# Routing of a two-layer decoder trunk: LayerNorm sums by VectorE, statistics and logits with tokens on partitions

## The reference

```python
h = _layer_norm(ALPHA * h + mix, ln_mix_g[layer], ln_mix_b[layer])   # mean, variance over the 1024 features
scores = jax.nn.sigmoid(jnp.einsum('bld,de->ble', h, w_router))      # 64 experts
biased = scores + router_bias
# 8 groups of 8 experts, the best 4 groups by the sum of their two best, the best 8 experts in them
w = ROUTED_SCALE * w / jnp.sum(w, axis=-1, keepdims=True)            # gates of the 8 chosen
```

## Time and profile before

| | us |
|---|---|
| median of 3 runs | 1601.27 |
| lowest, highest | 1598.33, 1609.75 |
| the profiled execution, its own time | 1615.54 |
| its span in the profile | 1613.8 |

### The profile page before, as it was taken

One profiled execution on the slowest core, in us unless ns is written; L12 is line 12 of the kernel. 1 busy time (PEld: TensorE's weight loads), 2 busy tenths in 40 slices (PEclk: granted clock), 3 DMA queues, 4 the chain that ended last, 5 costly groups with the idle time before them and its releaser, 6 DMA issues. The chain is left out here.

```text
span 1613.8 us, 24656 instructions
## 1 busy us (share of the span) xinstructions
PE 1461.5 (91%) x9414; PEld 864.6 (54%) x9414; DVE 691.3 (43%) x1471; ACT 355.4 (22%) x744; POOL 249.7 (15%) x323
## 2 busy tenths in 40 slices
PE   8999888999898999897999877987999997979996
PEld 6788668887544444353545466863434342424442
DVE  3889747631533343342434258043233332323323
ACT  3766454220410111110111020132011111111111
POOL 5779525200100000000000000001000000000000
PEclk9999999799899999898999978987999998989999
DMA  7679361039389999999999881395999999999994
GB/s 271 208 189 258 129 162 55 2 132 367 142 339 419 423 423 422 425 422 424 420 422 423 365 301 72 129 384 188 363 423 425 422 425 423 423 423 420 426 422 192
DMA packets 101490, 512.46 MB, mean 318 GB/s; under 512 B 36836, under 2 KB 42020, under 8 KB 66300
## 3 DMA queue, kind: packets, MB, share of 16 engines
q1 hardware_dynamic: 91548, 481.81, 75.3%
q0 software_dynamic: 9824, 29.05, 4.9%
HBM read 508.92 MB, written 17.10 MB: 326 GB/s over the span
## 5 line engine op out<-in xcount | busy, mean ns | idle before, releaser
L1986 DVE TENSOR_TENSOR e_ac<-e_sl,banks 128x256 f32<-128x256 f32 x54 | 22.7, 421 | 408.5 <-ACT e_sl L1895 408.5
L1774 PE MATMUL banks<-upper,e_xgT 128*64 128x512 f32 (+1 forms) x864 | 195.5, 612 | 1.3 <-issue 1.1
L304 PE MATMUL banks<-hT,dense_ring 128*128 128x272 f32 x768 | 184.9, 399 | 5.3 <-DMA dense_ring<-in_w_in 5.3
L1381 POOL DMA_INDIRECT x_xg<-rows_dram,x_idx x54 | 53.6, 993 | 848.6 <-DVE x_idx L1373 842.2
L1774 PE MATMUL banks<-dense_ring,e_xgT 128*64 128x512 f32 (+1 forms) x320 | 149.5, 623 | 38.3 <-issue 37.2
L304 PEld LDWEIGHTS banks<-hT,dense_ring 128*128 128x128 f32 x768 | 147.5, 193 | 39.3 <-DMA dense_ring<-in_w_in 5.3
L1774 PE MATMUL banks<-experts,e_xgT 128*64 128x512 f32 (+1 forms) x704 | 153.4, 608 | 0.9 <-issue 0.9
L1774 PEld LDWEIGHTS banks<-dense_ring,e_xgT 128*64 128x64 f32 (+1 forms) x320 | 41.1, 131 | 134.5 <-issue 132.5
L1895 ACT ACTIVATE e_sl<-banks 128x256 f32<-128x256 f32 x54 | 20.8, 385 | 402.4 <-PE banks L1774 402.4
L1792 PE MATMUL banks<-x_sg,route_consts 128*128 128x272 f32 x432 | 104.5, 394 | 2.8 <-ACT route_consts L1910 1.4
L1774 PEld LDWEIGHTS banks<-upper,e_xgT 128*64 128x64 f32 (+1 forms) x864 | 65.1, 132 | 74.4 <-issue 74.4
(11 more groups left out here) (453 smaller groups left out, 2179.0 us busy)
## 6 DMA issues: line engine op xcount, KB each, us to landing
upper<-in_moe_gate_up SPq DMA_DIRECT2D x54, 2048.0 KB, 25.2
experts<-in_moe_gate_up SPq DMA_DIRECT2D x44, 2048.0 KB, 26.9
upper<-in_moe_down SPq DMA_DIRECT2D x44, 1024.0 KB, 25.2
experts<-in_moe_down SPq DMA_DIRECT2D x44, 1024.0 KB, 26.2
dense_ring<-in_moe_down SPq DMA_DIRECT2D x40, 1024.0 KB, 25.0
dense_ring<-in_moe_gate_up SPq DMA_DIRECT2D x20, 2048.0 KB, 15.0
dense_ring<-in_w_in SPq DMA_DIRECT2D x47, 512.0 KB, 4.6
x_gate_up<-in_moe_gate_up SPq DMA_DIRECT2D x10, 2048.0 KB, 19.2
```

The costliest lines, as they stand in the source:

```text
L304: mm = pe.matmul(ps[g % 4][:, 0:T], slot[:, n % SLOTS_IN, c, :], hT[:, c, :], start=(c == 0), stop=(c == DC - 1))
L1381: pool.indirect_dma_start(out=ex["xg"][:, i % 2, :], out_offset=None, in_=mem["rows_dram"], in_offset=bass.IndirectOffsetOnAxis(ap=ex["idx ...
L1774: mm = pe.matmul(gub[e * n:(e + 1) * n, :], xgT[:, i % 2, c, e * n:(e + 1) * n], gate_up_weights(mem, j)[:, c, :], start=(c == 0), stop=(c ...
L1986: dve.tensor_tensor(ac[:], sl[:], gub[:, FF:], ALU.mult).then_inc(mul, 1)
```

## The change

Layer statistics move ahead: while the mixer's last projection runs, ScalarE squares each finished tile and VectorE adds up tiles and squares elementwise (`tally`, two adds per tile, one tile behind). The column sums go. The router's weight product, its column sum and its bias row are made in the same stage, on GpSimd and TensorE. In the routing stage TensorE sums over partitions with the token sums as the stationary operand, so mean, variance and root are columns of NT numbers per partition. The logits take the raw `hT` tiles as the stationary operand (128 loaded columns, 64 moving), and a ninth matmul takes off the mean's part. The reciprocal roots are spread by a matmul of ones with a diagonal. VectorE centres and scales the tiles afterwards, from PSUM.

```diff
@@ group_mixers, tensor
-                def column_sum(m): ...
                 for m in range(DC):
                     project(m, 1)
-                    if m >= 2:
-                        column_sum(m - 2)
-                column_sum(DC - 2)
-                column_sum(DC - 1)
+                    if m == 5:
+                        sum_router(pe, mem, 0)
+                    if m == 6:
+                        spread_bias(pe, mem, 0)
@@ scalar: wait added(m); square_tile(m); keep_router at m == 5.  gpsimd, last: weigh_router
@@ vector
                 for m in range(DC):
                     residual(m, 1)
+                    if m >= 2:
+                        dve.wait_ge(added, DC + m)
+                        tally(dve, mem, squares, squared, tallied, m - 1, T)
+                dve.wait_ge(added, 2 * DC)
+                tally(dve, mem, squares, squared, tallied, DC - 1, T)
@@ new functions
+def sum_router(pe, mem, layer):
+    wg, out = routing_scratch(mem, 2)["wg"], mem["bank"][7]
+    pe.wait_ge(mem["router_weighed"], layer + 1)
+    for c in range(DC):
+        pe.matmul(out[:, E:2 * E], mem["ones"][:], wg[:, c, :], start=(c == 0), stop=(c == DC - 1))
+    for c in range(DC):
+        shift = mem["ln_par"][:, (4 * layer + 1) * DC + c:(4 * layer + 1) * DC + c + 1]
+        mm = pe.matmul(out[0:1, 2 * E:3 * E], shift, mem["router_w"][:, c, :], start=(c == 0), stop=(c == DC - 1))
+    mm.then_inc(mem["router_summed"], 1)
+def spread_bias(pe, mem, layer):
+    pe.wait_ge(mem["router_kept"], 2 * (layer + 1))
+    pe.matmul(mem["bank"][7][:, 0:E], mem["ones"][0:1, :], routing_scratch(mem, 2)["bias_row"], start=True, stop=True)
+def tally(dve, mem, squares, squared, tallied, m, W):
+    sums, sqs, hN = mem["token_sums"][:, 0, 0:W], mem["token_sums"][:, 1, 0:W], mem["hT"][:, :, T - W:]
+    if m > 1:
+        dve.wait_ge(tallied, 2 * (m - 1))
+    dve.tensor_tensor(sums, hN[:, 0, :] if m == 1 else sums, hN[:, m, :], ALU.add).then_inc(tallied, 1)
+    dve.wait_ge(squared, m + 1)
+    dve.tensor_tensor(sqs, squares[:, 0, :] if m == 1 else sqs, squares[:, m % 2, :], ALU.add).then_inc(tallied, 1)
@@ norm_and_route, tensor (the squares' sums, 64 x W logits, bias matmuls and score turns go)
+                for tt, (t0, n) in enumerate(tiles):
+                    pe.matmul(stat_ps[0:n, tt:tt + 1], sums[:, t0:t0 + n], ones[:, 0:1], start=True, stop=True)
+                    mm = pe.matmul(stat_ps[0:n, NT + tt:NT + tt + 1], sqs[:, t0:t0 + n], ones[:, 0:1], start=True, stop=True)
+                mm.then_inc(totalled, 1)
+                pe.matmul(mean_ps[:, 0:W], ones[:], sums, start=True, stop=True).then_inc(mean_in, 1)
+                for tt, (t0, n) in enumerate(tiles):
+                    for c in range(DC):
+                        pe.matmul(lg_ps[0:n, tt * E:(tt + 1) * E], hN[:, c, t0:t0 + n], wg[:, c, :], start=(c == 0),
+                                  stop=False)
+                    mm = pe.matmul(lg_ps[0:n, tt * E:(tt + 1) * E], sums[:, t0:t0 + n], wg_sum, start=False, stop=True)
                 mm.then_inc(logits, 1)
+                pe.wait_ge(turned, 1)
+                for tt, (t0, n) in enumerate(tiles):
+                    mm = pe.matmul(rstd_ps[:, t0:t0 + n], ones[0:n, :], diag[0:n, tt, 0:n], start=True, stop=True)
+                mm.then_inc(rstd_in, 1)
@@ norm_and_route, scalar (eight squares and the 128 x W root go)
+                act.activation(warm[:], eps[0:1, 0:1], ACT.Sqrt).then_inc(warmed, 1)
+                act.copy(bias, bias_ps[:, 0:E]).then_inc(biased, 1)
+                act.wait_ge(varied, 1)
+                act.activation(var[:], var[:], ACT.Sqrt).then_inc(rooted, 1)
+                act.wait_ge(warmed, 1)
                 act.activation(warm[:], eps[0:1, 0:1], ACT.Sigmoid).then_inc(warmed, 1)
                 act.wait_ge(logit_in, 1)
+                act.activation(sc, sc, ACT.Sigmoid).then_inc(scored, 1)
@@ norm_and_route, vector, in its new order
+                dve.wait_ge(totalled, 1)
+                (four small operations, linked: minus mean, its square, variance, floor and epsilon)
+                dve.wait_ge(rooted, 1)
+                (reciprocal of [P, NT]; one diagonal per token tile)
+                dve.wait_ge(biased, 1)
+                dve.wait_ge(logits, 1)
+                (one scalar_tensor_tensor of n x 64 per token tile: logits * root + bias, then logit_in)
+                dve.wait_ge(mean_in, 1)
                 for c in range(0, 4):
+                    centre(c)
+                dve.wait_ge(scored, 1)
                 link(dve.tensor_tensor(bi[:], sc, rb[:].unsqueeze(1).broadcast_to([P, NT, E]), ALU.add))
                 (the eight-best searches, as before)
+                dve.wait_ge(rstd_in, 1)
+                for c in range(0, 4):
+                    scale(c)
+                for c in range(4, DC):
+                    centre(c)
                 for c in range(4, DC):
                     scale(c)
@@ norm_and_route, gpsimd: the product of router weights and gain goes (to weigh_router)
@@ norm_and_route, tensor: the wait for rows_c 3 ahead of the turn of selection and gates goes
@@ s5_mixer: the column sums go; sum_router after tile 13, spread_bias after tile 14, weigh_router on GpSimd,
   square_tile and keep_router on ScalarE, tally on VectorE, as in layer 0; gate_up_5 is allocated ahead of the stage
```

More of the change, by code:

```diff
@@ L920, in _ @@
                     roots(i + 1)
+                for m in range(DC):
+                    act.wait_ge(added, DC + m + 1)
+                    square_tile(act, mem, squares, squared, tallied, m, T)
+                    if m == 5:
+                        keep_router(act, mem, 0)
             @block.gpsimd
@@ L1401, in norm_and_route @@
         key_ps, sort_ps = bank[5], bank[3]
-        sq, mean, rstd = mem["acc"][:, :, 0:W], sb("mean", [P, W]), sb("rstd", [P, W])
+        sums, sqs = mem["token_sums"][:, 0, 0:W], mem["token_sums"][:, 1, 0:W]
         rows = rows_of(mem["acc"], 2)
@@ L1405, in norm_and_route @@
         row_tile = lambda tt: rows[:, tt, :] if tt < 2 else tail[:]
[L1406 to L1409, removed]
+        rb, after, lower = (mem[n] for n in ("router_b", "after", "lower"))
+        wg, wg_sum, diag, sc, bias = (routing_scratch(mem, NT)[n] for n in ("wg", "wg_sum", "diag", "scores", "bias"))
+        neg_mean, mean_sq, var, rstd = (sb(n, [P, NT]) for n in ("neg_mean", "mean_sq", "var", "rstd"))
         bi, mb, mr = (sb(n, [P, NT, E]) for n in ("bi", "mb", "mr"))
@@ L1564, in _ @@
                 link = step.done
-                dve.tensor_scalar(mean[:], sums[:, 0:W], 1.0 / D, None, ALU.mult).then_inc(meaned, 1)
-                dve.wait_ge(meaned, 1)
-                for c in range(DC):
-                    dve.tensor_tensor(hN[:, c, :], hN[:, c, :], mean[:], ALU.subtract).then_inc(centred, 1)
-                def scale(c):
-                    dve.tensor_tensor(hN[:, c, :], hN[:, c, :], rstd[:], ALU.mult).then_inc(scaled, 1)
-                dve.wait_ge(sd_ready, 1)
@@ new lines, in _ @@
+                ins.then_inc(turned, 1)
+                dve.wait_ge(biased, 1)
+                dve.wait_ge(logits, 1)
+                for tt, (t0, n) in enumerate(tiles):
+                    ins = dve.scalar_tensor_tensor(out=sc[0:n, tt, :], in0=lg_ps[0:n, tt * E:(tt + 1) * E],
+                                                   scalar=rstd[0:n, tt:tt + 1], in1=bias[0:n, :], op0=ALU.mult,
+                                                   op1=ALU.add)
+                ins.then_inc(logit_in, 1)
@@ L2678, in _ @@
                 def _(pe):
-                    def column_sum(m):
-                        pe.wait_ge(added, m + 1)
-                        pe.matmul(sums[:, 0:W], mem["ones"][:], hN[:, m, :], start=(m == 0), stop=(m == DC - 1))
                     for m in range(2 * DC):
```

122 lines of the change are left out of this document (67 added, 55 removed).

## The result

The changed kernel took 1620.51 us (median of 18 runs, 1612.87 to 1626.26) beside 1609.20 for the kernel before (18 runs on the same chip, 1598.33 to 1619.69). The ratio of the two is 1.0072, 95% interval 1.0056 to 1.0088: +11.6 us, with 9 to 14 as its ends. Forecast were +3.1 us and 1604.3, range 1595 to 1613. The measured time lies outside the range, for two reasons that should be kept apart: the median of before was 7.9 us above the one of three runs that the forecast started from, and the change cost 8.5 us more than forecast.

A forecast was written before the change was run, and what follows sets the result against it. No engine's busy time alone was taken as the bound; the chain through the routing stages' rows was. Layer 0's +3.95 and layer 1's -0.85 us made +3.1, so 1604.3 us for the median, range 1595 to 1613.

The forecast's parts named there:

- the price of the 128-column instruction: Float32 matmul with 128 loaded and few moving columns, in statistics, logits and router's sums: 0.12 us at both clocks.
- the end of 0.20: Upper price per 128-column instruction in the routing stage at half clock, load and matmul in series; 0.074 was the lower.
- rival (b): Serial loads: each 128-column load stands before its matmul at half clock in statistics and logits; 1612.6 us, chance 0.15.
- 0.16 for the router's sums at full clock: Upper price per instruction of the router's sums in the mixers: +0.65 us in each layer.
- the pause at the barrier: TensorE idle some 3 us after the last projection, so half clock was assumed at both routing stages' start.
- Layer 0's stage: Routing stage of layer 0: fourth normal at 15.1 us where before 13.3, plus 0.45 for turns, +2.25.
- Layer 1's stage: Routing stage of layer 1: fourth normal at 12.5 us where before 15.2, -2.7.
- the mixers' ends: Later last projection (1.05 us) and longer tail of adds: routing starts 1.7 us later in layer 0, 1.85 in layer 1.
- the second normals wait for ScalarE's copies: Routing stage of layer 0: the second normals start when ScalarE's copies end, not when VectorE's scaled tiles are ready.
- the turns at half clock: Layer 0's first row turns at half clock: 1.20 us to the first copy where it was 0.74, +0.45.
- rival (c): Absorbed: the experts' weight stream ends at its own time and takes up routing's shift; 1601.3 us, chance 0.1.
- The base: Starting time of the forecast: the median of the runs shown, 14.3 us below the profiled execution's 1615.54.

The follow-up runs named there:

- experiment 5: Changed kernel with logits summed with experts on partitions (64 router columns loaded, all tokens moving), then copied and turned, in both layers: ratio 1.0029 to the kernel before.
- experiment 3: Changed kernel with four idle matmuls of all tokens behind the last projection of both mixers, to fill TensorE's pause: ratio 1.0070 to the kernel before.
- experiment 7: Changed kernel with idle wide matmuls in TensorE's pauses of the routing stage: ratio 1.0040 to the kernel before.
- experiment 11: Changed kernel with router's sums and bias behind the last projection, adds before residuals, scales before searches, wide logits and idle wide matmuls: ratio 1.0020 to the kernel before.
- experiment 10: Kernel before, with layer 1's first ranked expert load held until the first gather has landed: ratio 1.0027 to the unedited kernel before.

## Why the prediction was wrong

- **The step that failed is the price of the 128-column instruction.** The forecast took "0.12, the row nearest in shape, for both clocks". It is 0.118 at full clock (sixteen in 1.89) and 0.213 at half (sixteen in 3.41), even a little over the end of 0.20. The row that was taken, four loads in 0.50 at half clock, loads 16 rows and moves 16 columns, and its price does not carry over to 128 rows and 64 columns. A row of the right shape was not in the trace of before, but a nearer one was, the turns of rows (128 loaded, 128 moving): 1.06 / 8 = 0.13 at full clock, and at half clock (windows 418 to 426 of before read 0.50) 2.82 / 12 = 0.235. Timeline of the kernel before, layer 0:

```profile
420.79 2.82 PE L1491 MATMUL banks<-ident,hT 128*128 128x128 f32 x12 [3.21 <-ACT hT L1530]
```

The forecast charged these turns for the half clock (1.20 to the first copy for 0.74) and not the logits, though half clock had been assumed for the start of both stages in the same text. With 0.20 the forecast gave 1612.6, +11.3, and measured are +11.6. The prediction's estimate from the Trainium skill ("TensorE: Matmul & The Clock Gate", LDWEIGHTS, for the 107 ns) is 0.160 for the full clock; its 53 ns for 64 moving columns are what that page has for the low clock. The trace has 0.118 at full clock and 0.213 at half, so the estimate fits neither.
- **So rival (b)'s price came true in the routing stage,** 0.213 for its 0.20. Its chance was 0.15. Its mechanism, a load and its matmul one after the other, did not: at half clock 128 loaded columns take 0.213 with one moving column as with 64, so the moving part adds nothing. Nor did its 0.16 for the router's sums at full clock, measured 0.118. That its total is so near (+11.3 beside +11.6) is luck: 1.3 us of it for those sums were not paid, and 1.5 us behind the rank were not in it.
- **How long the clock would stay low was not asked.** Nothing in the text said when it would rise in the logits, and 0.12 "for both clocks" made it look harmless. In layer 0 TensorE was busy without a pause for 9 us and the clock did not rise, and it was at half through layer 1's front too. In experiment 5, with wide matmuls in the same place, it came back. (The trace models the ends of matmuls, so "busy" here says that instructions stood without a gap, not how much of the array worked.) The Trainium skill ("TensorE: Matmul & The Clock Gate", What's actually happening) says that activity releases the throttle; in these 9 us of short instructions the trace does not show it, with the wide ones it does.
- **Right reason for the low clock?** No. The forecast put it down to the pause at the barrier and had it from the start of both stages. In layer 0 the clock was full at the start (statistics 0.11 apart) and fell 1.9 us into the stage, and filling most of the pause changed nothing there (experiment 3).
- **Layer 0's stage:** +2.25 forecast, +6.8 measured: the logits +4.0 over the forecast less 0.7 that the statistics and mean took less, and 1.5 behind the rank, a term not in the sum at all: the shared expert's first eight instructions at half clock (3.79 for 2.10).
- **Layer 1's stage:** -2.7 forecast, +1.2 measured by the normals in the first pair of profiles, and +0.1 at least in any pair; the sign was wrong. In the first pair 36 instructions at 0.093 more are 3.3 of the 3.9 missed, and the statistics and the mean 0.9 (2.7 for 1.8); the searches and normals behind them took 0.4 less than forecast.
- **Right:** the mixers' ends (+1.7 and +1.85 forecast, +1.9 and +2.1 measured), with router's sums of 2.94 and a tail of 2.04; that the second normals wait for ScalarE's copies; the turns at half clock (+0.45; 1.20 for 0.74); that all passes to the end, so that rival (c) fell; that nothing came near 1% faster.
- **The base:** the median of three runs, 1601.27, though the profiled execution of the same kernel had taken 1615.54. The text noted the 14.3 and drew nothing from it. Of 18 runs on one chip the median was 1609.2. A range of 18 us around a figure that could be 8 off by itself was too narrow. (A slip in the sum that nothing hangs on: with 0.074 for every 128-column instruction layer 0's term is -2.1 and not -2.5, since 22 of its 66 instructions load 16 columns.)

## What to carry to other kernels

Here a float32 instruction with 128 loaded and up to 64 moving columns cost the same whatever it moved, and 1.8 times as much at half clock (0.213 for 0.118). Price such an instruction at both levels, from a row of the same shape, before trading few wide matmuls for many short ones; the number of them counts, not the elements. And an edit that is right by itself can move the low stretch of the clock onto other work, so read the windows behind the edit too.

## What the runs showed of the hardware that was not expected

- 128 columns loaded cost 0.213 us at half clock whether one column moves (statistics of layer 1) or 64 (its logits), and 0.118 with 64 at full clock.
- TensorE shown busy without a pause for 9 us kept a granted clock of 0.50 with such instructions. With loads of 64 and 272 moving columns it was back at 1.00 at 5.3 us from the stage's start.
- Idle matmuls do raise the granted clock (experiment 7) but do not keep it up for good: in experiment 11 it fell 21 us into the stage, behind a window of 4 us with TensorE busy 1.85, and stayed at half for 13.6 us.
- Where the low stretch falls is part of the time: layer 0's stage took 30.3 us in two executions of its old form, and 32.9 in a third, in which the clock was at half for 17 us and not 10, until the shared expert had begun (experiment 10).
